# Two transformer blocks on one core: pool products among the queries, a merge gate within the attention, splits ahead of a merge's last eviction, cross queries ahead of the values

## What is computed

```python
# first block
merged = g[:, :, 0] * p_a + g[:, :, 1] * p_b + g[:, :, 2] * p_c
x = x + gate_m * (merged @ w_out[l])

def mixer_block(h, ...):                       # second block, per layer
    u = h @ w_in
    u_conv, q, k, v, u_pool, gates = jnp.split(u, SPLITS, axis=-1)
    y_conv = conv_branch(u_conv, ...)          # GLU, 31-tap depthwise conv, layer norm, silu, product
    y_attn = diff_attention(q, k, v, ...) @ attn_o     # 8 heads of 2 maps, rms norm (sub-layer norm)
    y_pool = pool_branch(u_pool, pool_w, pool_scale, pool_o)
    g = jax.nn.sigmoid(gates.reshape(B, S, 3, D))
    merged = g[:, :, 0] * y_conv + g[:, :, 1] * y_attn + g[:, :, 2] * y_pool
    return merged @ w_out

def pool_branch(u, w_grp, scale, w_o):         # four groups of 256 columns, windows 2, 4, 8, 16
    ...                                        # pooled = running mean over the window, less u
    y = jnp.einsum('bsgc,gcd->bsgd', pooled, w_grp).reshape(B, S, POOL_D) * scale
    return y @ w_o

def cross_attention(h, mem_n, wq, wkv, wo):    # 4 heads of 256, memory of 256 rows
    q = (h @ wq).reshape(B, S, X_HEADS, X_HEAD_DIM)
    k, v = jnp.split(mem_n @ wkv, 2, axis=-1)
    p = jax.nn.softmax(logits * X_HEAD_DIM ** -0.5, axis=-1)
    return (p @ v) @ wo

# a layer: x += 0.5*norm(ffn(norm(x))); x += norm(mixer(norm(x)));
#          x += norm(cross(norm(x), norm(mem))); x += 0.5*norm(ffn(norm(x)))
```

## Time and profile before

| | us |
|---|---|
| median of three runs | 2292.97 |
| the three runs | 2292.57, 2292.97, 2297.14 |
| the profiled execution | 2300.36 |
| its span | 2298.6 |

### The profile page before, as it was taken

How to read it: one execution, slowest core, us unless ns; L and a number is a source line. 1 busy time by engine, 2 the same in 40 slices (tenths; PEclk the granted TensorE clock), 3 DMA queues, 4 the chain that set the end, 5 groups by cost and what they waited for, 6 DMA issues and landing times.

```text
span 2298.6 us, 43655 instructions
## 1 busy us (share of the span) xinstructions
PE 2176.2 (95%) x17856; PEld 2113.8 (92%) x17856; DVE 1695.2 (74%) x2698; ACT 1200.2 (52%) x1894; POOL 102.6 (4%) x104
## 2 busy tenths in 40 slices
...
GB/s 311 278 156 129 175 174 258 148 190 195 222 191 197 195 217 186 110 121 150 189 196 125 168 204 190 176 203 192 217 184 159 115 133 153 228 156 122 209 180 132
DMA packets 401190, 415.62 MB, mean 181 GB/s; under 512 B 18526, under 2 KB 389632, under 8 KB 400353
## 3 DMA queue, kind: packets, MB, share of 16 engines
...
## 4 chain that ended last, share of the span: by engine, by line
PE 67%; DVE 23%; ACT 6%; issue 4%; DMA 1%; SPq 0%; DVEq 0%; ACTq 0%
PE gemm_ps L1022 44%; PE gemm_ps L1025 16%; DVE weights_lo L1701 8%; DVE x_res L2207 5%; ACT weights_hi L1267 1%; ACT e L1495 1%; DMA raw_weights<-in_xattn_kv_dram 1%; DVE neg_max L1966 1%; DVE h_lo L1874 1%; DVE mod_partial L1834 1%; PE misc_ps L1201 1%; PE misc_ps L1164 1%; DVE y L1910 1%; PE gemm_ps L1005 0%; PE misc_ps L1184 0%
## 5 line engine op out<-in xcount | busy, mean ns | idle before, releaser
L1701 DVE TENSOR_TENSOR weights_lo<-raw_weights,weights_hi 128x1024 fp32r<-128x1024 f32 (+1 forms) x704 | 835.8, 1200 | 347.5 <-ACT weights_hi L1267 344.2
L1267 ACT CAST weights_hi<-raw_weights 128x1024 fp32r<-128x1024 f32 (+1 forms) x704 | 717.0, 1032 | 587.6 <-PE gemm_ps L1022 411.8
L1022 PE MATMUL gemm_ps<-h_hi,weights_hi 128*128 128x256 f32 x3280 | 929.4, 283 | 15.8 <-DVE weights_lo L1701 5.5
L1022 PE MATMUL gemm_ps<-h_lo,weights_hi 128*128 128x256 f32 x3280 | 914.1, 279 | 0.0
L1022 PE MATMUL gemm_ps<-h_hi,weights_lo 128*128 128x256 f32 x3280 | 914.0, 279 | 0.0
L1022 PEld LDWEIGHTS gemm_ps<-h_hi,weights_hi 128*128 128x128 f32 x3280 | 621.9, 190 | 26.4 <-issue 15.7
L1022 PEld LDWEIGHTS gemm_ps<-h_lo,weights_hi 128*128 128x128 f32 x3280 | 619.6, 189 | 2.8 <-issue 2.4
L1022 PEld LDWEIGHTS gemm_ps<-h_hi,weights_lo 128*128 128x128 f32 x3280 | 619.7, 189 | 0.0
L2207 DVE SCALAR_TENSOR_TENSOR x_res<-zp,param_cols,x_res 128x256 f32<-128x256 f32 x480 | 197.1, 484 | 0.0
L1025 PE MATMUL gemm_ps<-weights_hi,hidh 128*128 128x256 f32 x688 | 189.9, 276 | 0.0
L1025 PE MATMUL gemm_ps<-weights_hi,hidl 128*128 128x256 f32 x688 | 189.9, 276 | 0.0
...
## 6 DMA issues: line engine op xcount, KB each, us to landing
raw_weights<-in_ffn_w_dram SPq DMA_DIRECT2D x256, 512.0 KB, 4.4
...
```

The costliest lines, as they stand in the source:

```text
L1022: mm = pe.matmul(ps[:, c, 0:T], w[:, m, kt, c * P:(c + 1) * P], x[:, f, :], start=start, stop=stop_)
L1267: act.copy(unit_of(WH, m % SPLIT, u), unit_of(RAWB, u["raw"] % RAW, u)).then_inc(sems["weights_rounded"], 1)
L1701: dve.tensor_tensor(unit_of(WL, m % SPLIT, u), unit_of(RAWB, u["raw"] % RAW, u), unit_of(WH, m % SPLIT, u), ALU.subtract).then_inc(sems["w ...
```

## The change

At the end of both merges (`merge_c` and the mixer's last merge) the last eviction is taken out of the list and put back two steps before its end, so that the splits of slices 0 to 5 are issued ahead of it and those of 6 and 7 behind; the `warm` matmuls of block 1 go, and `log_exp` follows the splits. In `queries_pool` each product with `pool_w` follows its window by one query instead of all four standing at the end. Gate 4 is issued within the attention, behind the merge of the pool branch, and `merge_attention` leaves it out. At the entry of the cross attention the first unit of values 0 stands in the place of the `warm` matmuls, the turns of slices 4 to 7 hang in the second unit of values 0 and the first of queries 0, and `x_row` follows that unit. The further queries come ahead of the values, and all are spread over twelve slots of the heads. The matmuls of the products, and the splits of the weights, are as many as before.

```diff
--- before.py
+++ after.py
@@ -195,7 +195,7 @@
         add("stat", key=key, s=s)
         add("rstd", key=key, s=s, out="RX")
 
-    def enter(key, name, at_):
+    def enter(key, name, at_, ahead=None):
 
 
         res = pending.pop()
@@ -213,7 +213,10 @@
         s = new_stat()
         k = dict(key=key, v=xv[0])
         h = dict(buf="H", gen=key, src="turned", ft0=0, after=readers.get("H"), v=xv[0], col=(name, at_))
-        add("warm", n=10)
+        if ahead:
+            S.append(ahead)
+        else:
+            add("warm", n=10)
         add("update_x", p=0, **res)
         add("update_x", p=1, **res)
         for f in range(4):
@@ -224,11 +227,15 @@
                 add("update_x", p=3, **res)
             for f in (2 * p, 2 * p + 1):
                 add("split", f=f, **h)
-        turns_of_h[0] = [None, None, dict(k, f=4), dict(k, f=5)]
-        turns_of_h[1] = [dict(k, f=6), dict(k, f=7), None, None]
         add("x_rstd_tok", key=key, v=xv[0])
         add("row_wide", key=key)
-        row_due.append(("x_row", dict(key=key, s=s)))
+        if ahead:
+            turns_of_h[0] = [None, dict(k, f=6), None, dict(k, f=7)]
+            row_next.append(("x_row", dict(key=key, s=s)))
+        else:
+            turns_of_h[0] = [None, None, dict(k, f=4), dict(k, f=5)]
+            turns_of_h[1] = [dict(k, f=6), dict(k, f=7), None, None]
+            row_due.append(("x_row", dict(key=key, s=s)))
 
     def attention(cfg, n):
 
@@ -457,13 +464,14 @@
     def merge_c():
         split("G", "oc", "qc", fts=4, ft0=4)
         branch(2, "oc")
+        last_evac = S.pop()
+        split("H", "b1m", "MG", mg=("b1", 2), half=True)
+        S.insert(len(S) - 2, last_evac)
     rest += collect(merge_c)
 
     begin = [i for i, (kind, _) in enumerate(rest) if kind == "unit"][20]
     S += rest[:begin] + spread(rest[begin:], mod_slots(range(NF, 20)))
     add("log_exp")
-    add("warm", n=7)
-    split("H", "b1m", "MG", mg=("b1", 2), half=True)
     for c in range(4):
         gemm("w_out", c * COLS, NF, ("H", "b1m"), "evac_y", ft=2 * c, sq=None, yk="b1r")
     residual("b1r", "gate_mod", chunk=2)
@@ -544,27 +552,37 @@
             def window(g):
                 add("window", l=l, g=g, gen=key + "p", after=after, s=new_stat())
 
+            def product(g):
+                gemm("pool_w", 0, 2, ("G", key + "p"), "evac_pool_w", ft0=2 * g, l=l, g=g)
+
             inputs(2)
             query(1)
             window(3)
             inputs(0)
             window(2)
+            product(3)
             query(2)
             window(1)
+            product(2)
             query(3)
             window(0)
-            for g in (3, 2, 1, 0):
-                gemm("pool_w", 0, 2, ("G", key + "p"), "evac_pool_w", ft0=2 * g, l=l, g=g)
+            product(1)
+            product(0)
             merge(0, 8, "pool_o", "q", True)
-
-        def merge(b, gate, w, gen, first):
+            gate(4)
+
+        def gate(n):
+            z2(l, "gates", n, "evac_gate", scaled=True, ft=2 * (n % 4))
+
+        def merge(b, gates, w, gen, first, gated=0):
             for c in range(4):
-                z2(l, "gates", gate + c, "evac_gate", scaled=True, ft=2 * c)
+                if c >= gated:
+                    gate(gates + c)
                 gemm(w, c * COLS, NF, ("G", key + gen), "evac_branch", l=l, ft=2 * c, first_branch=first, mg=(key, b))
 
         def merge_attention():
             split("G", key + "a", "q")
-            merge(1, 4, "attn_o", "a", False)
+            merge(1, 4, "attn_o", "a", False, gated=1)
 
         def conv(features):
 
@@ -583,8 +601,10 @@
         S.extend(spread(last[half:], norm))
         split("G", key + "c", "TMP", half=True)
         merge(2, 0, "conv_pw", "c", False)
+        last_evac = S.pop()
+        split("H", key + "o", "MG", mg=(key, 2), half=True)
+        S.insert(len(S) - 2, last_evac)
         add("log_exp")
-        split("H", key + "o", "MG", mg=(key, 2), half=True)
         mem = f"l{l}cm"
         add("mem_load", l=l, after=("split", "H", key + "o", 7))
         for c in range(4):
@@ -596,7 +616,6 @@
 
     def cross(l):
         key, mem = f"l{l}c", f"l{l}cm"
-        enter(key, f"norm{l}", 32)
 
         def values(j):
             gemm("xattn_kv", D + j * COLS, NF, ("M", mem), "evac_v2", form="T", l=l, dst="xv", c0=j * COLS)
@@ -605,15 +624,17 @@
             gemm("xattn_q", j * COLS, NF, ("H", key), "evac_scaled", l=l, dst="xq", ft=2 * j, by=(D // 4) ** -0.5)
 
 
-        values(0)
+        turns_of_h[1] = [None, dict(key=key, v=xv[0], f=4), None, dict(key=key, v=xv[0], f=5)]
+        first_values = collect(lambda: values(0))
+        enter(key, f"norm{l}", 32, ahead=first_values[0])
+        S.extend(first_values[1:])
         add("gain", key=key, l=l, row=5, tile="c", after=("unit", readers["M"]))
         queries(0)
         heads = attention(f"cross{l}", 4)
-        main = collect(lambda: (queries(1), values(1), queries(2), values(2), queries(3)))
-        S.extend(spread(main, heads[:7]))
-        S.extend(heads[7] + heads[8] + heads[9] + heads[10])
-        values(3)
-        for steps_ in heads[11:]:
+        main = collect(lambda: (queries(1), queries(2), values(1), queries(3), values(2), values(3)))
+        evicted = lambda kind, k: kind in ("evac_scaled", "evac_v2")
+        S.extend(spread(main, heads[:12], evicted))
+        for steps_ in heads[12:]:
             S.extend(steps_)
         split("H", key + "o", "xq")
         for c in range(4):
```

## The result

| | before | changed |
|---|---|---|
| median, us (7 runs each) | 2297.48 | 2320.61 |
| lowest to highest | 2292.57 to 2304.49 | 2312.72 to 2333.51 |
| ratio, 95% interval | | 1.0098, 1.0077 to 1.0120 |
| span of the profiled run | 2298.6 | 2325.9 |

The changed kernel is slower by 1.0%, some 22.5 us. The forecast was slower by 8.0, with a range to 2311; 2320.6 lies above it. The sign was right, the size was not. Of the 19.6 us between 2301.0 and 2320.6, 4.5 are in the base: the forecast added to the median of three runs, 2293.0, and the seven runs have 2297.5.

What follows compares the result with a forecast made beforehand. VectorE was taken to bound the mixer up to the convolution's end, TensorE the stretch from there on. Terms of -9.6 and +17.6 gave +8.0 on 2293.0, so 2301.0 us, range 2285 to 2311.

Steps and rivals of the forecast that it cites:

- A: End of block 1's merge: splits ahead of the last eviction let TensorE start `w_out` earlier, -1.5 us.
- B: End of the mixer, both layers: splits ahead of the eviction cut TensorE's 1.93 us wait, -3.7, and -1.7 of clock.
- F: Cross attention, both layers: queries ahead of values spare two of three waits for `pt`, -2.7 us in all.
- the -1.7: End of one layer's mixer: the half-clock stretch behind the 1.93 idle goes, 0 to 1.7 us gained once.
- E: Entry of the cross attention, both layers: late `y` and late wide row idle TensorE, +6.0 us, and +1.4 of clock.
- half of 1.4 each, +1.4: Cross-attention entry, both layers: idle times of 3.1 may bring a half clock, counted as half of 1.4 us each.
- Rival (3): Clock stays at 0.50 longer than 3.4 us after idle at entries and D, 1.75 more each: 2308.0; chance 0.15.
- D: First merge gate ahead of the splits, both layers: TensorE idles 4.3, convolution's mean 2.1 late; +4.2 us, +2.8 of clock.
- C: Pool products among the queries, both layers: VectorE waits longer at the first norm, +1.6 us a layer, +3.2 in all.
- The 2.0: First sub-layer norm: VectorE has by its order about 2.0 us more to do before its `q`; wait 2.2 becomes 3.8.

Runs made afterwards that it cites:

- A, B and F alone: The changed kernel with the pool products, gate 4 and the cross-attention entry taken back: 0.9952 of the kernel before, 11 us faster.
- C alone: Pool products among the queries, added to A, B and F alone: 0.9982 of the kernel before.
- D alone: Gate 4 moved into the attention, ahead of the splits, added to A, B and F alone: 1.0024 of the kernel before.
- D's second measurement: D alone run again, unchanged: 1.0053 of the kernel before.

## Why the prediction was wrong in size

**A: right.** -1.0 for -1.5. The eviction and the last two splits kept ahead of TensorE.

**B: right.** The wait went from 1.93 to 0.16, and in layer 1 the stretch before it from 82.5 to 80.7. In layer 0, whose 83.7 became 80.7, 1.2 more went; it is in the pace of the matmuls, below. The half clock behind the start of `w_out_2` is gone in the changed kernel and in every kernel of the experiments. But in A, B and F alone and in four others layer 0 has 3.4 us of it a little later, behind the idle time of 1.61 or 1.84 ahead of the cross attention's turns, where the kernel before has none behind 1.61. So the -1.7 is not shown as a gain that stays: from `w_out_2` to `x_row` layer 0 takes 38.9 in A, B and F for 39.7.

**F: right.** Two of three waits are gone, 1.6 to 2.2 a layer for 1.4.

**E: the mechanism right, the clock's term mis-sized.** The delay of `y` by 2.2, the idle times of 3.02 and 2.91 and the wait for the wide row are as worked out. The step that failed was "half of 1.4 each, +1.4": not one stretch of 3.4 us in every second case, but 10.2 us of half clock in each layer, beginning at the first turns and again at `x_row`, which also put the turns of slices 4 to 7 further apart (slice 7 came 10.4 behind the first turns, for the 8.7 of the sum). E measured +12.4 by the times and +10.0 by the rest of the layers, for +7.4. Rival (3) had this mechanism and put 3.5 on the two entries, where 2.6 to 5.0 came; its other half, a longer half clock at D, did not come (3.4 us in both layers of the changed kernel).

**C: right in kind, its two terms both off.** +2.2 in each mixer for +1.6, by the wait that was named; 6.9 by the times, 3.2 forecast. The idle time ahead of query 2 was 3.2 for 3.3. But the norm's matmul came 2.3 late and not 3.6, since 12 matmuls fewer stand ahead of it, and with C alone VectorE had no 2.0 more to do ahead of its `q`: the same 150 taps and 46 low parts, 132.8 us busy from `x_row` to there for 133.2. The 2.0 was counted in the order of the changed kernel, in which D's spread had moved the norm too. The two errors cancelled in part, so part of this term's nearness is luck.

**D: the step that failed.** The forecast took D for a change at the end of the attention, and costed its tail at 3.5 a layer ("+4.2, and +2.8 of clock"), which the trace gives as 3.1 and the times leave open. It put the spread at nothing, without asking what `spread` does when the list has two more units: all heads and norms move to later units on TensorE, VectorE does not get as much more to do in front of them, and it waits at all four norms for `rstd_q`. That was 5 us a layer by the profiles and up to 8 by the times, 10 to 16 of the 22.5. D alone measured 16.6 for 7.0. The order of the instructions could have told it: the first and the last norm were compared in it, the second and third were not, and for D not even the first.

The sum with the measured parts, by ratios: -11.0 + 6.9 + 16.6 + 12.4 = +24.9, for +22.5 measured with all of them (interval 17.7 to 27.6). Against their forecasts D cost 9.6 more, E 5.0 more, C 3.7 more, and A, B and F gained 1.4 more. The parts add within the intervals; with D's second measurement, 1.0053 on another chip, the sum would be some 6.7 higher.

The rule of the Trainium skill on table loads ("ScalarE: Activation LUTs", "Table sets: the hidden batching unit"), one load for a logarithm followed by an exponential, was rightly set aside. With D alone the last norm has two loads of 1.28 each, at 1058.00 and 1060.90 of its trace, the second of them in the chain that TensorE's 4.53 waits for.
